# Sliding-window attention of a two-block transformer: value product with the values stationary, two heads in column halves

## The reference, cut to what matters

```python
s_band = jnp.where(mask, s_band, NEG_INF_2)
s_sink = jnp.broadcast_to(sink_g[None, :, :, None, None], s_meta.shape[:-1] + (1,))
p = jax.nn.softmax(jnp.concatenate([s_band, s_meta, s_sink], axis=-1), axis=-1)
return (jnp.einsum('bhgqk,bkhd->bqhgd', p_band, vb)
        + jnp.einsum('bhgqm,bmhd->bqhgd', p_meta, v_meta))
```

## Time and profile before

| | us |
|---|---|
| median of 3 runs | 888.32 (886.84 to 890.65) |
| the profiled execution | 884.68 |
| its span, first to last instruction | 882.9 |
| TensorE busy | 829.7 (94%) |
| DVE busy | 554.1 (63%) |
| ScalarE busy | 471.4 (53%) |
| GpSimd busy | 122.4 (14%) |
| mean granted clock of TensorE | 0.979 |

### The profile page before, as it was taken

How to read it: one execution, slowest core, us unless ns; L and a number is a source line. 1 busy time by engine, 2 the same in 40 slices (tenths; PEclk the granted TensorE clock), 3 DMA queues, 4 the chain that set the end, 5 groups by cost and what they waited for, 6 DMA issues and landing times.

```text
span 882.9 us, 13033 instructions
## 1 busy us (share of the span) xinstructions
PE 829.7 (94%) x4350; PEld 684.0 (77%) x4350; DVE 554.1 (63%) x854; ACT 471.4 (53%) x962; POOL 122.4 (14%) x198
## 2 busy tenths in 40 slices
PE   7799999999999999699989999999998999999995
PEld 5678878777776787589878888888886788888884
DVE  5476667676777676756555665766566555455453
ACT  5476565375775554645555566555535544344343
POOL 0200121000232310153222524200000000000000
PEclk9999999999999999799999999999999899999999
DMA  9944543466676454652212434546664556656641
GB/s 268 268 139 128 146 120 122 141 177 205 193 216 184 139 161 120 174 143 83 63 55 71 127 108 126 166 145 208 204 202 138 186 182 193 209 155 197 207 137 48
DMA packets 147584, 138.13 MB, mean 156 GB/s; under 512 B 15184, under 2 KB 115680, under 8 KB 147520
## 3 DMA queue, kind: packets, MB, share of 16 engines
q1 hardware_dynamic: 145440, 130.21, 48.5%
q0 software_dynamic: 2080, 7.09, 2.8%
HBM read 136.22 MB, written 1.05 MB: 155 GB/s over the span
## 4 chain that ended last, share of the span: by engine, by line
PE 45%; ACT 4%; DVE 3%; issue 1%; ACTq 0%; DVEq 0%
PE psum L1059 38%; PE psum L1025 3%; PE psum L1142 2%; ACT probs L1406 2%; ACT w_hi L1294 1%; PE psum L1252 1%; DVE stats L1571 1%; DVE w_lo L1461 1%; PE psum L1255 1%; ACT xn L1316 0%; ACT gtmp L1436 0%; DVE xn L1500 0%; DVE x L1504 0%; ACT hstat L1439 0%; DVE o_st L1625 0%
## 5 line engine op out<-in xcount | busy, mean ns | idle before, releaser
L1461 DVE TENSOR_TENSOR w_lo<-raw,w_hi 128x1024 fp32r<-128x1024 f32 (+1 forms) x254 | 296.9, 1183 | 139.1 <-ACT w_hi L1294 82.3
L1294 ACT ACTIVATE w_hi<-raw 128x1024 fp32r<-128x1024 f32 (+1 forms) x254 | 253.0, 1015 | 70.7 <-PE psum L1059 47.2
L1059 PE MATMUL psum<-w_hi,h_hi 128*128 128x512 f32 (+1 forms) x656 | 262.8, 401 | 13.0 <-DVE h_lo L1510 10.3
L1059 PE MATMUL psum<-w_lo,h_hi 128*128 128x512 f32 (+1 forms) x656 | 248.8, 379 | 0.0
L1059 PE MATMUL psum<-w_hi,h_lo 128*128 128x512 f32 (+1 forms) x656 | 248.5, 379 | 0.0
L1059 PEld LDWEIGHTS psum<-w_hi,h_hi 128*128 128x128 f32 x656 | 125.7, 192 | 36.0 <-issue 15.8
L1059 PEld LDWEIGHTS psum<-w_lo,h_hi 128*128 128x128 f32 x656 | 125.1, 191 | 19.8
L1059 PEld LDWEIGHTS psum<-w_hi,h_lo 128*128 128x128 f32 x656 | 126.0, 192 | 16.2
L1406 ACT ACTIVATE probs<-psum,stats 128x272 f32<-128x272 f32 (+2 forms) x104 | 47.6, 467 | 87.4 <-DVE stats L1563 30.2
L1059 PE MATMUL psum<-w_hi,m_hi 128*128 128x512 f32 x152 | 60.0, 395 | 2.4 <-DVE m_lo L1510 1.7
L1059 PE MATMUL psum<-w_lo,m_hi 128*128 128x512 f32 x152 | 59.2, 390 | 0.0
(11 more groups left out here) (158 smaller groups left out, 1053.0 us busy)
## 6 DMA issues: line engine op xcount, KB each, us to landing
raw<-in_w_in SPq DMA_DIRECT2D x112, 256.0 KB, 3.5
raw<-in_w_in SPq DMA_DIRECT2D x44, 512.0 KB, 4.4
raw<-in_w_ffn_in SPq DMA_DIRECT2D x88, 256.0 KB, 3.9
raw<-in_w_out SPq DMA_DIRECT2D x24, 512.0 KB, 3.4
raw<-in_w_in SPq DMA_DIRECT2D x64, 192.0 KB, 2.7
raw<-in_w_ffn_out SPq DMA_DIRECT2D x22, 512.0 KB, 4.6
raw<-in_w_mem_kv SPq DMA_DIRECT2D x8, 512.0 KB, 3.8
raw<-in_w_branch_swa SPq DMA_DIRECT2D x8, 512.0 KB, 3.3
```

Of the source, the lines that this page charges most:

```text
L1059: last = nc.tensor.matmul(psum[:, bank, 0:n], sx[name][:, c, t * P:(t + 1) * P], wx[:, u["slot"], kk, 0:n], start=u["first"] and kk == 0 a ...
L1294: nc.scalar.activation(w_hi[:, u["slot"], :, 0:n], raw[:, u["raw"], :, 0:n], ACT.Copy)\
L1461: nc.vector.tensor_tensor(w_lo[:, u["slot"], :, 0:n], raw[:, u["raw"], :, 0:n], w_hi[:, u["slot"], :, 0:n].bitcast(F32), ALU.subtract)\
```

## The change

The swa heads are handled in pairs after the exponentials, and their product gives its result already turned.

- The maximum of both heads is one reduction over four rows, and the two operations with the sink are done for both at once; ScalarE's exponentials of either head wait for that.
- A new step, scale (places 5.75 and 7.75), adds the sink's terms, takes the reciprocals and multiplies the probabilities of both heads by them in one DVE operation. turn_p waits for it.
- turn_p of both heads stands at 6.4 (8.4) and turns only the 128x128 blocks.
- A new step, turn_tm (7 and 9), turns the meta columns of both heads into one ring bank; ScalarE copies them to p_tm in one operation of 512 elements.
- out_t (7.5 and 9.5) takes the place of out: the values are stationary (64 columns), the turned probabilities of 256 queries move, and the two heads write to partitions 0 to 63 and 64 to 127 of one ring bank. Three key blocks by two heads make six products, twelve passes.
- mix_t (7.9 and 9.9) splits that bank straight into mix_hi (ScalarE) and mix_lo (DVE), 256 columns a pair. turn_mix and the evictions to o_st are gone for swa.
- The scores of swa no longer wait for the p_tm copy of the pair before.

Counters, semaphores (scaled, tm_ready) and the branches of "out" and "turn_mix" that only lose their swa case are left out below.

```diff
@@ -153,8 +153,8 @@
                 out=(5.75, 6.75, 7.75, 8.75), turn_mix=(11.5,)),
-    "swa": dict(turn_qk=(3.25, 2.75), scores=(4.5, 4.5, 6.5, 6.5), turn_p=(5.5, 6, 7.5, 8),
-                out=(6.25, 7, 8.25, 9), turn_mix=(10.5,)),
+    "swa": dict(turn_qk=(3.25, 2.75), scores=(4.5, 4.5, 6.5, 6.5), scale=(5.75, 7.75), turn_p=(6.4, 6.4, 8.4, 8.4),
+                turn_tm=(7, 9), out_t=(7.5, 9.5), mix_t=(7.9, 9.9)),
     "diff": dict(turn_qk=(1.5, 2.5), scores=(4.25, 4.25), blend=(6.25,), turn_p=(7.75,), out=(8.75,),
...
@@ -354,11 +357,35 @@
             probs_reader[s["j"] % 4] = ("tp_done", s["batch"] + 1)
-            if g["kind"] in ("swa", "diff"):
+            if g["kind"] == "diff":
                 meta_turned[s["j"] % 2] = s["pt"] + 1
+        elif what == "scale":
+            s["scaled"] = pl.next("scales")
+            for h in s["heads"]:
+                h["scaled"] = s["scaled"]
+        elif what == "turn_tm":
+            s["batch"] = pl.next("batches") - 1
+            s["tm"] = pl.next("tms")
+            ring(s, ("tm_ready", s["tm"]))
+            assert s["heads"][0]["pt"] % 2 == 0 and s["heads"][1]["pt"] == s["heads"][0]["pt"] + 1
+            for h in s["heads"]:
+                probs_reader[h["j"] % 4] = ("tp_done", s["batch"] + 1)
+        elif what == "out_t":
+            s["o"] = pl.next("outs") - 1
+            s["out_free"] = ["turned", None]
+            ring(s, s["out_free"], "out_")
+            g["last_out"] = s["o"] + 1
+            outs_of_pt.extend([s["o"] + 1] * 2)
+        elif what == "mix_t":
+            s["hi"] = pl.next("his")
+            s["turned"] = s["out_free"][1] = pl.next("turns")
+            name, c = g["mix"][s["c"]]
+            last = [reader[p]["u"] + 1 for p in [(name, c, t) for t in range(NT)] if p in reader]
+            s["dest_free"] = ("unit_used", max(last)) if last else None
         elif what == "out":
             s["o"] = pl.next("outs") - 1
-            ring(s, ("out_used", s["o"] + 1), "out_")
+            g["last_used"] = pl.next("used")
+            ring(s, ("out_used", g["last_used"]), "out_")
             if g["kind"] == "mem":
...
@@ -1210,17 +1245,44 @@
                         pe.wait_ge(blended, s["blended"])
+                    elif kind == "swa":
+                        pe.wait_ge(scaled, s["scaled"])
                     else:
...
                     pr = probs[:, j % 4]
-                    blocks = [(0, 0), (1, 0), (1, 1)] if kind == "mb" else [(0, 0), (0, 1), (1, 0), (1, 1)]
+                    blocks = [(0, 0), (1, 0), (1, 1)] if kind == "mb" else \
+                        [(0, 0), (1, 0), (0, 1), (1, 1)] if kind == "swa" else [(0, 0), (0, 1), (1, 0), (1, 1)]
                     todo = [(psum[:, s["bank"], n * P:(n + 1) * P], pr[:, t, k * P:(k + 1) * P], P)
                             for n, (t, k) in enumerate(blocks)]
-                    if kind in ("swa", "diff"):
+                    if kind == "diff":
...
                     turn(todo)
+                elif what == "turn_tm":
+                    wait(pe, s["bank_free"])
+                    pe.wait_ge(scaled, s["scaled"])
+                    turn([(psum[0:META, s["bank"], (2 * n + t) * P:(2 * n + t + 1) * P],
+                           probs[:, h["j"] % 4, t, T:T + META], P)
+                          for n, h in enumerate(s["heads"]) for t in range(NT)])
+                elif what == "out_t":
+                    g = s["g"]
+                    vs = stage[:, g["ga"] % NSTAGE]
+                    v0 = KINDS["swa"]["v"]
+                    pe.wait_ge(pt_ready, s["heads"][1]["pt"] + 1)
+                    pe.wait_ge(tm_ready, s["tm"])
+                    wait(pe, s["out_bank_free"])
+                    keys = [(vs[:, kt, v0:v0 + DH], p_t, slice(kt * T, (kt + 1) * T)) for kt in range(NT)]
+                    keys.append((gflat[:, META_VA + g["kv"] * DH:META_VA + (g["kv"] + 1) * DH], p_tm, slice(0, T)))
+                    for n, (value, prob, at) in enumerate(keys):
+
+                        for i, h in enumerate(s["heads"]):
+                            last = nc.tensor.matmul(psum[DH * i:DH * (i + 1), s["out_bank"], 0:T], value,
+                                                    prob[:, h["pt"] % 2, at], start=(n == 0), stop=(n == 2),
+                                                    skip_group_check=True)
+                    last.then_inc(out_done, 1)
+                    for t in range(NT):
+                        where[g["mix"][s["c"]] + (t,)] = s["turned"]
                 elif what == "out":
...
@@ -1422,11 +1482,24 @@
                     last = nc.scalar.activation(p_t[:, s["pt"] % 2, 0:n], psum[:, s["bank"], 0:n], ACT.Copy)
-                    if kind in ("swa", "diff"):
+                    if kind == "diff":
                         b0 = 2 + 2 * (s["j"] % 2)
...
                     last.then_inc(pt_ready, 1)
+                elif what == "turn_tm":
+                    act.wait_ge(tp_done, s["batch"] + 1)
+                    if s["heads"][1]["pt"] >= 2:
+
+                        act.wait_ge(out_done, s["heads"][1]["pt_free"])
+                    nc.scalar.activation(p_tm[0:META].rearrange("p n q -> p (n q)"), psum[0:META, s["bank"], :],
+                                         ACT.Copy).then_inc(tm_ready, 1)
+                elif what == "mix_t":
+                    act.wait_ge(out_done, s["o"] + 1)
+                    wait(act, s["dest_free"])
+                    name, c = s["g"]["mix"][s["c"]]
+                    nc.scalar.activation(S_hi[name][:, c, :], psum[:, s["out_bank"], 0:T], ACT.Copy)\
+                        .then_inc(turned_hi, 1)
                 elif what == "out" and s["g"]["kind"] == "diff":
...
@@ -1554,6 +1627,24 @@
                         continue
+                    if kind == "swa":
+                        if "mate" not in s:
+                            continue
+                        dve.wait_ge(scores_done, j + 2)
+
+                        dve.wait_ge(probs_ready, j - 2)
+                        two = stats[:, j % 4:j % 4 + 2]
+                        hd = g["kv"] * 4 + s["a"]
+                        link(nc.vector.tensor_reduce(
+                            two[:, :, 0:2],
+                            psum[:, 2:6, 0:T + META].rearrange("p (h t) k -> p h t k", h=2), AX.X, ALU.max, negate=True))
+                        link(nc.vector.tensor_tensor(
+                            two[:, :, 0:2], two[:, :, 0:2],
+                            sinks[:, 16 + hd:18 + hd].unsqueeze(2).to_broadcast([P, 2, NT]), ALU.min))
+                        nc.vector.tensor_tensor(two[:, :, 4:6], two[:, :, 0:2],
+                                                sinks[:, hd:hd + 2].unsqueeze(2).to_broadcast([P, 2, NT]),
+                                                ALU.add).then_inc(negmax, 2)
+                        continue
                     dve.wait_ge(scores_done, j + 1)
...
@@ -1570,14 +1661,21 @@
                                                        negate=True)
-                        if kind == "swa":
-                            hd = g["kv"] * 4 + s["a"]
-                            link(last)
-                            link(nc.vector.tensor_scalar(stt[:, 0:2], stt[:, 0:2], sinks[:, 16 + hd:17 + hd], None,
-                                                         ALU.min))
-                            last = nc.vector.tensor_scalar(stt[:, 4:6], stt[:, 0:2], sinks[:, hd:hd + 1], None,
-                                                           ALU.add)
                     last.then_inc(negmax, 1)
+                elif what == "scale":
+                    j = s["heads"][0]["j"]
+                    dve.wait_ge(probs_ready, j + 2)
+                    two, inv = stats[:, j % 4:j % 4 + 2], rec[:, j % 4:j % 4 + 2, 0:NT]
+                    link(nc.vector.tensor_tensor(two[:, :, 2:4], two[:, :, 2:4], two[:, :, 6:8], ALU.add))
+                    link(nc.vector.reciprocal(inv, two[:, :, 2:4]))
+                    pr = probs[:, j % 4:j % 4 + 2]
+                    nc.vector.tensor_tensor(pr, pr, inv.unsqueeze(3).to_broadcast([P, 2, NT, T + META]), ALU.mult)\
+                        .then_inc(scaled, 1)
+                elif what == "mix_t":
+                    dve.wait_ge(turned_hi, s["hi"])
+                    name, c = s["g"]["mix"][s["c"]]
+                    nc.vector.tensor_tensor(S_lo[name][:, c, :], psum[:, s["out_bank"], 0:T],
+                                            S_hi[name][:, c, :].bitcast(F32), ALU.subtract).then_inc(turned, 1)
                 elif what == "blend":
...
@@ -1601,12 +1699,9 @@
-                        dve.wait_ge(tp_done, by_ga[g["ga"] - 2]["mixed"])
-                    if kind in ("mb", "mem", "swa"):
+                        dve.wait_ge(tp_done, mixed_before(g["ga"]))
+                    if kind in ("mb", "mem"):
                         dve.wait_ge(probs_ready, j + 1)
-                        if kind == "swa":
```

(23 more changed lines are left out.)

7 lines of the change are left out of this document (4 added, 3 removed).

## The result

The changed kernel takes 898.48 us (median of 4 runs, 897.33 to 902.32), the kernel before 887.58 us beside it (884.12 to 890.65). The ratio is 1.013, 95% interval 1.0096 to 1.0164: slower by 1.3%, where no measurable change was forecast, at 890.2 us within 880 to 897.

What follows compares the result with a forecast made beforehand. Bounds taken: TensorE's work and, close by, a loop over scores, DVE and ScalarE. From 884.68 us: -4.0 halves, +0.7 and +1.0 edges, +4.2 clock, net +1.9, 886.6; plus 3.6 for the median, 890.2 us, range 880 to 897.

Steps and rivals of the forecast that it cites:

- The column halves: In out_t on TensorE, two heads' passes overlap in separate halves: 1.6 us, between ends of 1.2 and 2.4.
- the prices: Costs of single new operations: out_t 1.6 us, DVE's reduction 1.3 and product 1.3, ScalarE's p_tm copy about 0.6.
- Rival B: In out_t, column halves pass one after the other, 2.4 us: 6.4 over the forecast, 896.6 us; chance 0.13.
- The first loop: Scores, reduction, exponentials, p_tm copy, out_t: out_t starts 4.75 us after scores end, stalling TensorE 2.1 or 1.2 us.
- Rival A: TensorE's sum of work stays the bound, each pair saving 1.2 us, 9.5 in all: median 878.8 us; chance 0.17.
- The half of 11.0 us: Interval from one swa pair's scores to the next: 10.9 and 11.1 us, mean 11.0, against 11.57 before.
- a gain of 4.0 us: Over seven swa halves between score matmuls: 77.0 us against 81.0 before.
- The second loop: After the exponentials, w_hi, w_lo, then scale before the turns: just covered, late by 0.1 to 0.5 us every second half.
- The clock: TensorE's granted clock drops to half after stalls: three low stretches for one before, adding 4.2 us.
- rival C: Stalls put TensorE at half clock in six or more stretches: +6.1 us, 894.4 us; chance 0.15.
- The edges: Ends of the swa stretch: first pair loses 0.7 us with a stall of nearly 4, last pair loses 1.0.

Runs made afterwards that it cites:

- e4: Changed kernel with both heads of a pair writing their product to one column half, half the swa output left out: 904.66 us in one run.
- e13: Kernel before with only the weight splits of diff parts issued ahead of the attention steps: 880.14 us, ratio 0.9900.
- e14: Changed kernel with only the weight splits of diff parts issued ahead of the attention steps: 895.86 us, ratio 1.0096 to the kernel before.
- e1: Changed kernel with turn_tm at 6.4 and 8.4, so p_tm is copied before the next scores: 902.44 us, ratio 1.0133 to the kernel before.
- e6: e1 with scale left out, so probabilities are not divided by their sums: 884.66 us, ratio 0.9944 to the kernel before.
- e12: Changed kernel with scale alone left out, turn_tm staying at 7 and 9: 892.78 us, ratio 1.0043 to the kernel before.
- e3: Changed kernel with dummy identity products in TensorE's waits, nothing taken away: 897.97 us, ratio 1.0089 to the kernel before.
- e7: Kernel before with each head's probabilities normalised before their turn, the product unchanged: 930.57 us, ratio 1.0445.

## Why the prediction was wrong, point by point

**The column halves and the prices were right.** Out_t was put at 1.6 us with its entry and took 1.44; the reduction at 1.3 and took 1.29 (415.91); the product at 1.3 and took 1.29 to 1.37; the p_tm copy at 0.6 and took 0.57. Rival B, passes one after another, is refuted by the changed kernel and, from the other side, by e4. The Trainium skill, TensorEngine Tiling (Array Packing), gives up to twice the speed for a dimension of at most 64, under Theoretical Speedup. The traces agree: two column halves gave a factor 1.9. Its rule under Key Properties, that a change of tiling mode drains TensorE, can have cost 0.24 us at most between 409.21 and 410.65: that is what 1.44 is over the 1.20 of two halves wholly at once.

**The first loop was right.** 4.75 us from the end of the scores to out_t was the sum. From the projection matmul behind the scores to out_t it is 431.85 - 427.00 = 4.85 in the fourth interval; in the third it is 421.05 - 415.68 = 5.37, with a small operation of DVE that took 0.73 us, and in the fifth 443.95 - 438.33 = 5.62. Rival A, TensorE's sum as the bound, fell with it.

**The half of 11.0 us was right for the third and fourth interval, at 11.3, and wrong for the rest.** This is the step that failed: I worked out one half in swa parts, multiplied it by seven, and set it against 11.57 us a half, an average over two kinds of parts with all stalls in it, for "a gain of 4.0 us". The seven intervals took 88.0 us where 77.0 were forecast, against 81.2 before. By kind of part, in us:

| intervals | 2 to 4 | 5 to 8 |
|---|---|---|
| forecast, halves of 11.0 | 33.0 | 44.0 |
| kernel before | 31.7 | 49.6 |
| changed kernel | 35.2 | 52.8 |
| e13, kernel before, splits first | 31.7 | 41.2 |
| e14, changed kernel, splits first | 35.1 | 46.8 |

In swa parts the kernel before needed 10.6 us a half, less than my 11.0: TensorE had no wait there, as the earlier trace rows had shown for 412 to 426 us, and a loop of 11.0 could only lose. The whole forecast gain lay in the later intervals, where the old half took 12.4 us, and 10.3 with the splits first (e13): 2.1 us of it came from the order of the weight splits, which the change leaves as it is. I also wrote that the projection splits keep their order. They keep it, but from 438 us on the parts are those of the diff groups, whose splits are issued behind the attention steps of their place (SPLIT_LAST, L51). There the split stands between the exponentials and the p_tm copy. ScalarE in the changed kernel, at 430 us and at 442 us (start, duration, operation):

```profile
431.13 0.57 ACT L1495 ACTIVATE p_tm<-psum 16x512 f32<-16x512 f32 x1
431.61 0.83 ACT L1354 ACTIVATE w_hi<-raw 128x768 fp32r<-128x768 f32 x1
```

```profile
442.54 0.85 ACT L1354 ACTIVATE w_hi<-raw 128x768 fp32r<-128x768 f32 x1
443.28 0.57 ACT L1495 ACTIVATE p_tm<-psum 16x512 f32<-16x512 f32 x1
```

So p_tm, and out_t with it, comes 0.75 us later, a stall of 2.81 instead of 2.1. The same order makes DVE copy the turned keys behind w_lo, behind w_hi, behind the exponentials; DVE there:

```profile
456.25 0.96 DVE L1534 TENSOR_TENSOR w_lo<-raw,w_hi 128x768 fp32r<-128x768 f32 x1 [3.08 <-ACT w_hi L1354]
457.12 0.43 DVE L1596 COPY qk<-psum 128x272 f32<-128x272 f32 x1
```

The split waits until 456.25 and the copy lands at 457.55, TensorE has stood still for 3.25 us, and this is the sixth interval, 15.9 us. Both waits were to be seen before the change: the qk wait of 1.8 us stood in the earlier trace rows, and the chain in the earlier trace rows, w_hi right behind the exponentials, is from another place with the same effect. The test is e14: without that order the fifth to eighth intervals fall from 52.8 to 46.8 us, 6.0 of the 8.8 by which they were over the forecast. In the median it is less, 898.5 to 895.9 us with overlapping ratios.

The order of the splits explains why the later halves missed 11.0 us. It does not explain why the changed kernel is slower than the one before: e13 gains more by the same edit than e14 does. That is the work of the two loops, which hold a half at 11 us and more where the old kernel's, with the splits first, takes 10.1 to 10.9.

**The second loop was undersized.** Scale was called just covered. It is, as long as out_t stalls: the waits for it were 0.34 and 0.35 us, the forecast 0.1 to 0.5. But it left no room, so that nothing of what e1 took away could be gained, and e6 and e12 show its weight: the pair of loops is worth 1.9%, either alone 0.9% or nothing. Its price in the later intervals shows only once p_tm is out of the way (e6 against e1); with p_tm in place it is the first pair's (e12). Also, in the third interval two tiny operations of DVE took 0.16 and 0.73 us where I had 0.45 for both with their gaps:

```profile
415.91 1.29 DVE L1638 TENSOR_REDUCE stats<-psum 128x4 f32<-128x1088 f32 x1 [1.29 <-PE psum L1177]
417.24 0.16 DVE L1641 TENSOR_TENSOR stats<-stats,sinks 128x4 f32<-128x4 f32 x1
417.50 0.73 DVE L1644 TENSOR_TENSOR stats<-stats,sinks 128x4 f32<-128x4 f32 x1
```

GpSimd was at work on the rotary embedding beside them; that this is why they are slow was not tried.

**The clock was right in kind and too small.** Three low stretches of 3.4 us were forecast, ten of 100 us at half clock; there were four, two of them of 7 us, 20 us in all. That is as much as the six of rival C, which had 0.15. It is no cause of its own: each dip came with a stall. What it costs was measured only in one execution, as at least 3.7 us of the stretch (e3).

**The edges.** The first pair's stall was forecast as nearly 4 us and was 4.6, and the interval took 12.2 us where 10.5 was worked out, since the turns behind that stall ran at half clock (eight transposes from 399.96 in 1.9 us, 1.0 at full clock). The last pair was forecast at 1.0 us of loss; its interval, the ninth, took 2.6 us more than before, with the p_t copies behind the diff exponentials.

The sum: for the eight intervals 87.7 us and 4.2 for the clock, 91.9, were forecast and 100.2 were measured. The wait for keys (3.2 against 1.8 before), three stalls of out_t 0.5 to 0.7 us over the forecast and the last 1.0 over it, and ten more microseconds at half clock are that difference in kind; the parts overlap too much to be added up.

## What to carry to other kernels

When a step is moved, work out its queue at every place at which it will run, not once: here the same list of steps ran in two kinds of parts, and the issue order of an unrelated step (a weight split) differed between them. Set the new interval against the old one at the same place, not against an average: the average held stalls that the change could not remove. A shorter product on the bound engine gives nothing while its operands come through two in-order engines: find all loops that start at the same event before costing one, since taking one away leaves the next. And give a candidate's side edit to the kernel before as well: the best version found here is no faster than the old kernel with the same one entry of a list changed.

## What the runs showed that was not expected

- Column halves of TensorE overlap in float32: twelve passes of 256 columns in 1.44 us, against 2.70 us in one half.
- Identity products in TensorE's waits held its granted clock up: 0.98 on average over 96.5 us instead of 0.90 over 100.2. The one low stretch left began in a wait that was not filled.
- Issuing the weight splits of eight groups ahead of the attention steps made the kernel before 1.0% faster (0.9862 to 0.9937); no form of the new product without this edit came below the kernel before, save one that leaves the normalisation out (0.9944).
- Normalising float32 probabilities on DVE ahead of their turn cost 4.5% in the kernel before (e7), and 0.9% or 1.9% in the changed one, as the p_tm wait stayed or was gone (e12, e6).
